# Stationary operands of the streamed products read with a step of two elements instead of one

## The chip, the core and the metric

The kernel runs on one core of a Trainium2 chip. The metric is the device time of one execution, in microseconds (us). The engines are TensorE (PE in the rows; PEld is its loading of stationary operands), VectorE (DVE), ScalarE (ACT), GpSimd (POOL) and SyncE (SP), which issues most of the DMAs. "Stationary operand" and "weights" mean the same below: the 128x128 block that TensorE holds while the columns of the moving operand stream past it.

## The reference

One inference step of a two-layer decoder, for a prompt of 256 tokens and 8 sequences of 4 new tokens (288 tokens in all), width 1024. Only the parts with streamed weights matter here:

```python
def mixer(h, st, lb, p):
    z = h @ p['w_in']
    ...
def peer(h, wq, k1, k2, u, v):
    ...
        sc, pos = lax.top_k(cand, PEER_TOPK)
        idx = jnp.take_along_axis(cidx, pos, axis=-1)
        gw = jax.nn.softmax(sc.astype(jnp.float32), axis=-1)
        act = jax.nn.gelu(jnp.einsum('thkd,td->thk', jnp.take(u, idx, axis=0), xb).astype(jnp.float32))
        return jnp.einsum('thk,thkd->td', (gw * act).astype(xb.dtype), jnp.take(v, idx, axis=0))
```

`peer_u` and `peer_v` have 16384 rows of 1024 floats for each layer. `w_in` has 26 blocks of 128 columns and 12 columns more.

## The kernel before

All weights come from one array in memory, `stream`, cut into tiles of 128 partitions by 1024 floats (512 KB). SyncE loads the tiles one after another into `ring` (three slots; the last stage has three more, `more_ring`). A loop over the two layers runs these stages in order: `project_block` (the product with `w_in`, 27 tiles, 288 moving columns), `local_block`, `hgrn_block` and `delta_block` (the three head groups), `output_block`, `experts_block` (128 tiles of `peer_u`; the prompt's 256 tokens are the moving columns, the result goes through gelu into a table of activations), `gates_block` (weights that table by the top-k gates) and `combine_block` (128 tiles of `peer_v`, moving operand the weighted activations of 128 experts for 256 tokens).

For the prompt, then, every expert is computed and the unwanted ones have gate zero. For the 32 sample tokens the wanted rows alone are gathered, by indirect DMAs from GpSimd, and VectorE multiplies and adds them; the sums stand in `m.tokens`, and 8 products with `m.folded` (line 2702) fold and turn them.

In `project_block`, `experts_block` and `combine_block` a float32 product is made of three products of type float32r. ScalarE copies half a tile (128x512) to `parts` as float32r, the high part (line 423 or 2631). VectorE or GpSimd writes what is left, the low part (line 430 or 2638). TensorE then multiplies: high weights by high and low moving operand (lines 473 and 2691), low weights by the high moving operand (lines 477 and 2695). `parts` has three places for a half tile, each with a high and a low side. Half a tile holds four chunks: chunk k is the 128x128 stationary operand for the k-th slice of the contraction (of the output, in `combine_block`). Each of the matmuls has its own load of a chunk, so each tile costs 24 loads and 24 matmuls.

Before the change chunk k of a half tile lies in 128 adjacent floats of each partition. The function `part` gives the view, and TensorE reads it with a step of one element. Each engine runs its instructions in the written order; semaphores join them (`hi_ready`, `lo_ready`, `done`, `parts_used`).

Of the kernel before, what the change touches and what calls it, by code (L numbers as in the profile page):

```python
# [27 lines left out]
P = 128  # L28
D = 1024
KD = D // P  # L30
DEPTH = 2
# [14 lines left out]
PARTS = 3  # L46
# [11 lines left out]
T_BETA = 0  # L58
T_IN = T_BETA + 1
T_LOCAL0 = T_IN + IN_TILES  # L60
# [5 lines left out]
T_U = T_QUERY + KD  # L66
T_V = T_U + NKEYS
T_X = T_V + NKEYS
# [44 lines left out]
NSAMP = NB * NS  # L113
# [284 lines left out]
def sum_column(pe, m, k, out):  # L398

    return pe.matmul(out, m.ones, m.square[:, k, :], start=(k == 0), stop=(k == KD - 1))  # L400
# [6 lines left out]

def part(m, q, side):

    return m.parts[:, q % PARTS, side, :].rearrange("p (k n) -> p k n", k=KD // 2)  # L410


def half_tile(m, t, half):
# [20 lines left out]
def wait_low(eng, m, s, first, g, j, half):  # L434

    t = first + j
    if half:
        eng.wait_ge(m.done[t % RING], g + (t // RING + 1))
    else:
        eng.wait_ge(s["lo_ready"], g * RING + (j + 1))  # L440


def each_tile(eng, first, end, body, ring=RING):

    assert first % ring == 0
    start, turns = first // ring, end // ring
    if turns - start == 1:
        for j in range(ring):
            body(start, j)
    elif turns > start:  # L450
        with eng.Fori(start, turns) as g:
            for j in range(ring):
                body(g, j)
    for n in range(turns * ring, end):
        body(turns, n % ring)


def split_product(pe, m, s, first, g, j, hr, out, tokens, columns=None):

    for half in range(2):
        hi, lo = part(m, 2 * j + half, 0), part(m, 2 * j + half, 1)
        pe.wait_ge(s["hi_ready"], g * 2 * RING + (2 * j + half + 1))
        for k in range(KD // 2):
            kk = half * KD // 2 + k
            if columns is not None:  # L470
                pe.wait_ge(columns, kk + 1)
            for side in range(2):
                pe.matmul(out, hi[:, k, :], hr[:, side, kk, 0:tokens], start=(kk + side == 0), stop=False)  # L473
        wait_low(pe, m, s, first, g, j, half)
        for k in range(KD // 2):
            kk = half * KD // 2 + k
            mm = pe.matmul(out, lo[:, k, :], hr[:, 0, kk, 0:tokens], start=False, stop=(kk == KD - 1))  # L477
        mm.then_inc(s["parts_used"], 1)


# [151 lines left out]
def project_block(nc, m, l, hr, stream, small_in, mixc_in, state_in):  # L632
# [7 lines left out]
    with signals(nc, m, names) as s, nc.psum_tensor("ps_z", [P, 4, 512], F32) as ps_z, \  # L640
# [101 lines left out]
        def _(v):  # L742
# [81 lines left out]
            for t in range(1, 1 + IN_TILES):  # L824
                for half in range(2):
                    split_low(v, m, s, T_BETA, 0, t, half)
                n = t - 1
                if n == CONV_AT - 2:
                    soft_in()
                elif n == CONV_AT:  # L830
                    v.wait_ge(s["pads_ready"], 4)
                if 0 <= n - CONV_AT < 4 * CONV:
                    part, k = (n - CONV_AT) // CONV, (n - CONV_AT) % CONV
                    v.wait_ge(s["z_out"], 3 * part + 4)
                    if part:
                        conv(m.yc, m.xc, range(3 * part - 3, 3 * part), k, m.par("dn_w"))
                    else:
                        conv(m.yb, m.xb, range(B_TILES), k, m.par("lru_w"), m.par("lru_b"))
                    if k == CONV - 1:
                        v.wait_ge(s["conv_step"], count[0])  # L840
                        v.sem_inc(s["conv_done"], 1)
                if n == CONV_AT + CONV:
                    v.tensor_copy(m.xcb[:, :, 0:NP], m.yb[:, :, 0:NP])
                    v.tensor_copy(batched(m.xcb[:, :, NP:NT]),
                                  m.yb[:, :, XP:XW].rearrange("p k (b s) -> p k b s", b=NB)[:, :, :, 0:NS])
                elif n == IN_TILES - 5:
                    soft_first()
                elif n == IN_TILES - 4:
                    soft_series(0, 3)
                elif n == IN_TILES - 3:  # L850
                    soft_series(3, len(LOG1P))
                elif n == IN_TILES - 2:
                    soft_last()
# [1344 lines left out]
def experts_block(nc, m, l, hr, stream, spots_in):  # L2198
# [7 lines left out]
    with signals(nc, m, names) as s, nc.psum_tensor("ps_s", [P, 4, 512], F32) as ps_s, \  # L2206
# [12 lines left out]
        def _(pe):  # L2219
            def tile(g, j):  # L2220
                pe.wait_ge(s["act_out"], g * RING + (j + 1))
                split_product(pe, m, s, T_U, g, j, hr, ps_u[:, j, 0:NP], NP)
# [368 lines left out]
def combine_block(nc, m, l, stream, u_rows):  # L2591

    AHEAD = 2
# [12 lines left out]
    with signals(nc, m, names) as s, \  # L2606
# [34 lines left out]
        def low_is_there(pe, g, j, half):  # L2641
            _, _, done, base = slot(j)
            if half:
                pe.wait_ge(done, g + (base + 1))
            else:
                pe.wait_ge(s["lo_ready"], g * VRING + (j + 1))

        def bank(n):
            return ps[:, 2 * n:2 * n + 2, :]
# [9 lines left out]
        @block.sync  # L2659
        def _(sp):  # L2660
            def load(g, j):
                tile, loaded, done, base = slot(j)
                sp.wait_ge(done, g + base)
                sp.dma_start(tile, stream[l, g * VRING + (T_V + j), :, :]).then_inc(loaded, 16)

            for j in range(RING, VRING):
                tile, loaded, _, _ = slot(j)
                sp.dma_start(tile, stream[l, T_V + j, :, :]).then_inc(loaded, 16)
            with sp.Fori(1, TURNS) as g:
                for j in range(VRING):  # L2670
                    load(g, j)
            for j in range(NKEYS % VRING):
                load(TURNS, j)

        @block.tensor
        def _(pe):
            pe.wait_ge(s["zeroed"], 1)
            for n in range(4):
                pe.matmul(bank(n), zeros[:, 0:P], zeros[:, :], start=True, stop=False)

            def tile(g, j):
                pe.wait_ge(s["act_hi"], g * VRING + (j + 1))
                for half in range(2):
                    q = (2 * j + half) % PARTS
                    hi, lo = part(m, q, 0), part(m, q, 1)
                    pe.wait_ge(s["hi_ready"], g * 2 * VRING + (2 * j + half + 1))
                    for side in range(2):
                        if side and half == 0:
                            pe.wait_ge(s["act_lo"], g * VRING + (j + 1))
                        for k in range(KD // 2):  # L2690
                            pe.matmul(ps[:, half * KD // 2 + k, :], hi[:, k, :], act_parts[:, j % AHEAD, side, :],  # L2691
                                      start=False, stop=False)
                    low_is_there(pe, g, j, half)
                    for k in range(KD // 2):
                        mm = pe.matmul(ps[:, half * KD // 2 + k, :], lo[:, k, :], act_parts[:, j % AHEAD, 0, :],  # L2695
                                       start=False, stop=False)
                    mm.then_inc(s["parts_used"], 1)

            each_tile(pe, 0, VRING * (TURNS - 1), tile, VRING)
            pe.wait_ge(s["samples_ready"], 1)  # L2700
            for k in range(KD):
                mm = pe.matmul(ps_m[:, NSAMP * k:NSAMP * (k + 1)], m.tokens[:, k * P:(k + 1) * P], m.folded,
                               start=True, stop=True)
            mm.then_inc(s["samples_summed"], 1)
            each_tile(pe, VRING * (TURNS - 1), NKEYS, tile, VRING)
            for n in range(4):
                pe.matmul(bank(n), zeros[:, 0:P], zeros[:, :], start=False, stop=True).then_inc(s["summed"], 1)
            for k in range(KD):
                pe.wait_ge(s["squares_ready"], k + 1)
                mm = sum_column(pe, m, k, ps_n[:, 0:NT])  # L2710
            mm.then_inc(s["sums_ready"], 1)
# [155 lines left out]
def host_layout(a):  # L2867
# [9 lines left out]
    stream = np.zeros((DEPTH, TILES, P, D), f)  # L2877
# [12 lines left out]
    out = a["w_out"].reshape(DEPTH, KD, P, 2, D // 2)[:, OUT_K].reshape(DEPTH, KD // 2, 2, P, 2, D // 2)  # L2890
    stream[:, T_OUT:T_QUERY] = out.transpose(0, 4, 1, 3, 2, 5).reshape(DEPTH, KD, P, D)
    stream[:, T_QUERY:T_U] = a["peer_wq"].reshape(DEPTH, KD, P, D)
    stream[:, T_U:T_V] = a["peer_u"].reshape(DEPTH, NKEYS, NKEYS, KD, P).transpose(0, 2, 4, 3, 1).reshape(DEPTH, NKEYS, P, D)
    stream[:, T_V:T_X] = a["peer_v"].reshape(DEPTH, NKEYS, NKEYS, D).transpose(0, 2, 1, 3)

    small = np.zeros((DEPTH, P, SMALL_W), f)

# [39 lines left out]
    j, i = np.arange(P)[:, None], np.arange(P)[None, :]  # L2937
# [89 lines left out]
```

## Time and profile before

| | |
|---|---|
| median of 3 runs | 2350.78 us (2343.35 to 2357.78) |
| the profiled execution's own time | 2358.03 us |
| its span, first to last instruction | 2356.1 us |
| mean granted TensorE clock | 0.971 of full |
| PE busy | 2249.4 us, 95% |
| PEld busy | 2085.2 us, 89% |
| DVE, ACT, POOL busy | 63%, 54%, 45% |

The profile describes one execution. Busy time of PE overlaps that of PEld, and neighbouring matmuls overlap each other, so that the mean duration of a matmul is longer than the time from one to the next. That distance is found from a stretch that holds nothing else: its length over the number of matmuls in it.

### The profile page before, as it was taken

The numbers are of one execution on the slowest core, as the hardware profiler recorded it, in microseconds if no ns is written. First come the engines' busy times: TensorE is split into PE (matmuls) and PEld (weight loads), VectorE is DVE, ScalarE is ACT, GpSimd is POOL, SyncE is SP. The second block draws the span as 40 slices with busy tenths as digits, with TensorE's granted clock in tenths as the row PEclk, the third lists the DMA queues.
The fourth block names the chain that finished last, engine by engine and source line by source line (L and its number), as shares of the span: only waits on it lengthen the run. The fifth ranks groups of instructions, "written<-read, shape, count | busy, mean of one in ns | idle before, by whom it ended". The sixth has DMA issues, their size and how long they took to land. (4 is left out here: it accounts for less than half of the span.)

```text
span 2356.1 us, 57811 instructions
## 1 busy us (share of the span) xinstructions
PE 2249.4 (95%) x20446; PEld 2085.2 (89%) x20478; DVE 1495.8 (63%) x3099; ACT 1271.2 (54%) x2439; POOL 1054.3 (45%) x960
## 2 busy tenths in 40 slices
PE   6979999999999999999989799999999999999998
PEld 4956779999998799999979377799999978999997
DVE  3756527963225968888666663499422287887885
ACT  3634215567557855555556431355765597555554
POOL 0021007874445746566300210288544474665661
PEclk9978899999999999999999789999999999999999
DMA  7462034555554179889644602355555533898993
GB/s 285 153 251 91 12 135 164 177 186 201 187 188 164 63 266 312 288 301 313 204 162 163 257 30 92 124 180 179 196 187 187 187 117 129 299 310 272 311 310 101
DMA packets 123814, 455.52 MB, mean 193 GB/s; under 512 B 13744, under 2 KB 14256, under 8 KB 122544
## 3 DMA queue, kind: packets, MB, share of 16 engines
q1 hardware_dynamic: 105264, 386.80, 46.4%
q0 software_dynamic: 18432, 67.12, 10.4%
q8 instruction: 78, 1.28, 0.2%
q14 instruction: 40, 0.33, 0.1%
HBM read 449.37 MB, written 4.49 MB: 193 GB/s over the span
## 5 line engine op out<-in xcount | busy, mean ns | idle before, releaser
L430 POOL TENSOR_TENSOR parts<-ring,parts 128x512 fp32r<-128x512 f32 x358 | 463.8, 1299 | 475.0 <-ACT parts L423 461.4
L423 ACT ACTIVATE parts<-ring 128x512 fp32r<-128x512 f32 x620 | 389.3, 632 | 348.4 <-PE ps_u L477 280.8
L473 PE MATMUL ps_u<-h_parts,parts 128*128 128x256 f32 x4096 | 563.0, 280 | 1.0 <-ACT parts L423 0.6
L2691 PE MATMUL ps_y<-act_parts,parts 128*128 128x256 f32 x4096 | 562.8, 279 | 0.0
L473 PEld LDWEIGHTS ps_u<-h_parts,parts 128*128 128x128 f32 x4096 | 514.4, 188 | 3.5 <-ACT parts L423 2.0
L2691 PEld LDWEIGHTS ps_y<-act_parts,parts 128*128 128x128 f32 x4096 | 515.1, 188 | 0.8 <-ACT parts L2631 0.7
L430 DVE TENSOR_TENSOR parts<-ring,parts 128x512 fp32r<-128x512 f32 x262 | 180.7, 693 | 372.0 <-ACT parts L423 350.5
L2740 POOL TENSOR_TENSOR act_parts<-big,act_parts 128x256 fp32r<-128x256 f32 x256 | 246.4, 962 | 303.5 <-ACT act_parts L2720 303.5
L477 PE MATMUL ps_u<-h_parts,parts 128*128 128x256 f32 x2048 | 322.2, 279 | 1.4 <-DVE parts L430 1.1
L2695 PE MATMUL ps_y<-act_parts,parts 128*128 128x256 f32 x2048 | 322.7, 279 | 0.0
L477 PEld LDWEIGHTS ps_u<-h_parts,parts 128*128 128x128 f32 x2048 | 275.4, 188 | 2.2 <-DVE parts L430 1.5
L2695 PEld LDWEIGHTS ps_y<-act_parts,parts 128*128 128x128 f32 x2048 | 275.5, 188 | 0.0
L2638 DVE TENSOR_TENSOR parts<-ring,parts 128x512 fp32r<-128x512 f32 x260 | 213.8, 845 | 74.1 <-ACT parts L2631 73.4
L2638 DVE TENSOR_TENSOR parts<-more_ring,parts 128x512 fp32r<-128x512 f32 x252 | 209.1, 849 | 73.7 <-ACT parts L2631 73.7
L2720 ACT ACTIVATE act_parts<-big 128x256 fp32r (+1 forms) x256 | 107.1, 418 | 220.4 <-PE ps_y L2695 211.0
L2631 ACT ACTIVATE parts<-ring 128x512 fp32r<-128x512 f32 x260 | 162.0, 624 | 49.9 <-PE ps_y L2695 49.9
L2631 ACT ACTIVATE parts<-more_ring 128x512 fp32r<-128x512 f32 x252 | 157.4, 625 | 45.8 <-PE ps_y L2695 45.8
L2526 POOL TENSOR_TENSOR onehot<-keep,sel 128x512 f32<-128x512 f32 x128 | 133.1, 1042 | 49.9 <-PE ps_g L2498 37.0
L2498 PEld LDWEIGHTS ps_g<-onehot 128*128 128x128 f32 x1024 | 135.6, 196 | 16.9 <-issue 13.2
L2498 PE MATMUL ps_g<-onehot 128*128 128x128 f32 x1024 | 140.6, 281 | 7.7 <-ACT onehot L2539 4.1
L473 PE MATMUL ps_z<-x_parts,parts 128*128 128x288 f32 x864 | 133.2, 296 | 4.5 <-ACT parts L423 4.5
L473 PEld LDWEIGHTS ps_z<-x_parts,parts 128*128 128x128 f32 x864 | 121.0, 188 | 5.8 <-ACT parts L423 5.4
(407 smaller groups left out, 2801.3 us busy)
## 6 DMA issues: line engine op xcount, KB each, us to landing
ring<-in_stream SPq DMA_DIRECT2D x506, 512.0 KB, 3.5
more_ring<-in_stream SPq DMA_DIRECT2D x126, 512.0 KB, 5.1
extra_ring<-in_stream SPq DMA_DIRECT2D x32, 512.0 KB, 5.4
mod_ring<-in_stream SPq DMA_DIRECT2D x32, 512.0 KB, 3.3
big<-in_stream SPq DMA_DIRECT2D x16, 512.0 KB, 11.6
out_state_out<-big SPq DMA_DIRECT2D x2, 1440.0 KB, 6.9
big<-in_state SPq DMA_DIRECT2D x2, 1280.0 KB, 10.6
big<-in_mixc SPq DMA_DIRECT2D x2, 1024.0 KB, 8.1
```

The costliest lines, as they stand in the source:

```text
L423: eng.activation(m.parts[:, q % PARTS, 0, :], half_tile(m, t, half), ACT.Copy).then_inc(s["hi_ready"], 1)
L430: eng.tensor_tensor(m.parts[:, q % PARTS, 1, :], half_tile(m, t, half), m.parts[:, q % PARTS, 0, :].bitcast(F32), ALU.subtract).then_inc(m ...
L473: pe.matmul(out, hi[:, k, :], hr[:, side, kk, 0:tokens], start=(kk + side == 0), stop=False)
L477: mm = pe.matmul(out, lo[:, k, :], hr[:, 0, kk, 0:tokens], start=False, stop=(kk == KD - 1))
L2498: mm = pe.matmul(ps_g[:, q % SETS, c, :], first[:, q % SETS, c, :], second[:, q % SETS, c, :], start=True, stop=True)
L2526: pool.tensor_tensor(second[:, g % SETS, :, :], spread(m.iota, 1, GROUP), spread(tokens_of(m.second_key, i, g), 2, P), ALU.subtract).then_ ...
L2631: act.activation(m.parts[:, q % PARTS, 0, :], tile[:, half * D // 2:(half + 1) * D // 2], ACT.Copy).then_inc(s["hi_ready"], 1)
L2638: v.tensor_tensor(m.parts[:, q % PARTS, 1, :], tile[:, half * D // 2:(half + 1) * D // 2], m.parts[:, q % PARTS, 0, :].bitcast(F32), ALU.s ...
L2691: pe.matmul(ps[:, half * KD // 2 + k, :], hi[:, k, :], act_parts[:, j % AHEAD, side, :], start=False, stop=False)
L2695: mm = pe.matmul(ps[:, half * KD // 2 + k, :], lo[:, k, :], act_parts[:, j % AHEAD, 0, :], start=False, stop=False)
L2720: act.activation(act_parts[:, j % AHEAD, 0, :], column(g, j), ACT.Copy).then_inc(s["act_hi"], 1)
L2740: pool.tensor_tensor(act_parts[:, j % AHEAD, 1, :], column(g, j), act_parts[:, j % AHEAD, 0, :].bitcast(F32), ALU.subtract).then_inc(s["ac ...
```

## The change

The host lays the streamed tiles of `w_in`, `peer_u` and `peer_v` out differently: the two chunks of a pair are interleaved, element by element. Where a partition held 128 floats of chunk 0 and then 128 of chunk 1, it now holds the first float of chunk 0, the first of chunk 1, the second of chunk 0, and so on. `part` returns the four chunks as views with a step of two floats. The copies that split a tile into high and low parts run over whole half tiles, with the same instructions as before, since the order inside does not matter to them; the tiles have the same size and the same loads. The gathered rows of `peer_v` come interleaved too, so that the sums in `m.tokens` are, and the last 8 products read them with the step of two (line 2702 before). `peer_u` rows for the gather come from another array and keep their order, and so do the other tiles (`w_out`, `peer_wq`, `w_ada`).

On no engine does the change add, drop or move an instruction; what differs is the access pattern of the stationary operands. In the kernel before, every one of them has a step of one element, or is four runs of 32 elements with that step (bfloat16).

```diff
 def part(m, q, side):
 
-    return m.parts[:, q % PARTS, side, :].rearrange("p (k n) -> p k n", k=KD // 2)
+    pairs = m.parts[:, q % PARTS, side, :].rearrange("p (j n b) -> p j n b", j=KD // 4, b=2)
+    return [pairs[:, k // 2, :, k % 2] for k in range(KD // 2)]
...
             for side in range(2):
-                pe.matmul(out, hi[:, k, :], hr[:, side, kk, 0:tokens], start=(kk + side == 0), stop=False)
+                pe.matmul(out, hi[k], hr[:, side, kk, 0:tokens], start=(kk + side == 0), stop=False)
...
-            mm = pe.matmul(out, lo[:, k, :], hr[:, 0, kk, 0:tokens], start=False, stop=(kk == KD - 1))
+            mm = pe.matmul(out, lo[k], hr[:, 0, kk, 0:tokens], start=False, stop=(kk == KD - 1))
...
+            tokens = m.tokens.rearrange("p (j n b) -> p j n b", j=KD // 2, b=2)
             for k in range(KD):
-                mm = pe.matmul(ps_m[:, NSAMP * k:NSAMP * (k + 1)], m.tokens[:, k * P:(k + 1) * P], m.folded,
+                mm = pe.matmul(ps_m[:, NSAMP * k:NSAMP * (k + 1)], tokens[:, k // 2, :, k % 2], m.folded,
                                start=True, stop=True)
...
+    for tiles in (slice(T_BETA, T_LOCAL0), slice(T_U, T_X)):
+        chunks = stream[:, tiles].reshape(DEPTH, -1, P, KD // 2, 2, P)
+        stream[:, tiles] = chunks.transpose(0, 1, 2, 3, 5, 4).reshape(DEPTH, -1, P, D)
```

The two products of `combine_block` change from `hi[:, k, :]` and `lo[:, k, :]` to `hi[k]` and `lo[k]` in the same way.

## Rows read from the trace of the kernel before

**Rows 1.** The page: busy time, share of the span and instructions of each engine

```profile
PE 2249.4 (95%) x20446; PEld 2085.2 (89%) x20478; DVE 1495.8 (63%) x3099; ACT 1271.2 (54%) x2439; POOL 1054.3 (45%) x960
```

**Rows 2.** Groups by line and form, PE: count, busy us, mean ns, idle us before

```profile
L473 PE MATMUL ps_u<-h_parts,parts 128*128 128x256 f32 x4096 | 563.0, 280 | 1.0 <-ACT parts L423 0.6
L2691 PE MATMUL ps_y<-act_parts,parts 128*128 128x256 f32 x4096 | 562.8, 279 | 0.0
L2695 PE MATMUL ps_y<-act_parts,parts 128*128 128x256 f32 x2048 | 322.7, 279 | 0.0
L477 PE MATMUL ps_u<-h_parts,parts 128*128 128x256 f32 x2048 | 322.2, 279 | 1.4 <-DVE parts L430 1.1
L473 PE MATMUL ps_z<-x_parts,parts 128*128 128x288 f32 x864 | 133.2, 296 | 4.5 <-ACT parts L423 4.5
L477 PE MATMUL ps_z<-x_parts,parts 128*128 128x288 f32 x432 | 75.4, 297 | 0.1
```

**Rows 3.** Busy us (x matmuls) in stretches of combine, project (layers 0, 1) and output

```profile
850.00:1150.00 300.00, 300.00 (x2572) 1.00 0.89 299
75.00:105.00 30.00, 30.00 (x229) 1.00 0.47 159
1215.00:1245.00 30.00, 30.00 (x228) 1.00 0.51 172
335.00:350.00 15.00, 15.00 (x63) 1.00 0.42 140
```

**Rows 4.** Groups by line and form, PEld: loads of 128, 32 and 12 columns

```profile
L2691 PEld LDWEIGHTS ps_y<-act_parts,parts 128*128 128x128 f32 x4096 | 515.1, 188 | 0.8 <-ACT parts L2631 0.7
...
L2254 PEld LDWEIGHTS ps_s<-keep,big 128*32 128x32 f32 x128 | 3.4, 110 | 0.3
...
L933 PEld LDWEIGHTS ps_q<-big 128*12 128x12 f32 x24 | 2.1, 92 | 3.8 <-issue 2.9
```

**Rows 5.** Timeline, PEld, 1161.5 to 1164.2 us: start us, length us, instructions

```profile
1161.93 1.87 PEld L2702 LDWEIGHTS ps_m<-keep,big 128*128 128x128 f32 x16
1163.72 0.65 PEld L2691 LDWEIGHTS ps_y<-act_parts,parts 128*128 128x128 f32 x5
```

**Rows 6.** Timeline, PE, same stretch: the matmuls of 32 columns to these loads

```profile
1162.05 1.87 PE L2702 MATMUL ps_m<-keep,big 128*128 128x32 f32 x16
```

**Rows 7.** Timeline, PE, 332 to 352 us: products of type f32 in the output stage

```profile
331.51 20.85 PE L2191 MATMUL ps_w<-big,ring 128*128 128x288 f32 x82
```

**Rows 8.** The page: groups that split the tiles, and what they wait for

```profile
L430 POOL TENSOR_TENSOR parts<-ring,parts 128x512 fp32r<-128x512 f32 x358 | 463.8, 1299 | 475.0 <-ACT parts L423 461.4
L423 ACT ACTIVATE parts<-ring 128x512 fp32r<-128x512 f32 x620 | 389.3, 632 | 348.4 <-PE ps_u L477 280.8
...
L2638 DVE TENSOR_TENSOR parts<-ring,parts 128x512 fp32r<-128x512 f32 x260 | 213.8, 845 | 74.1 <-ACT parts L2631 73.4
```

More of the change, by code:

```diff
@@ L2690, in tile @@
                         for k in range(KD // 2):
-                            pe.matmul(ps[:, half * KD // 2 + k, :], hi[:, k, :], act_parts[:, j % AHEAD, side, :],
+                            pe.matmul(ps[:, half * KD // 2 + k, :], hi[k], act_parts[:, j % AHEAD, side, :],
                                       start=False, stop=False)
@@ L2694, in tile @@
                     for k in range(KD // 2):
-                        mm = pe.matmul(ps[:, half * KD // 2 + k, :], lo[:, k, :], act_parts[:, j % AHEAD, 0, :],
+                        mm = pe.matmul(ps[:, half * KD // 2 + k, :], lo[k], act_parts[:, j % AHEAD, 0, :],
                                        start=False, stop=False)
```

## Prediction

> **What bounds the kernel now.** I began with the page's busy times [rows 1]: PE is busy for 95% of the span, PEld for 89%, and no other engine passes 63%. The groups by line and form come next [rows 2]. Two stages with the same form, 128x256, hold 4096+2048 matmuls in `experts_block` and as many in `combine_block`, 12288 together, and the project stage has 864+432 = 1296 of 288 columns. What the reader is to see there is the last column: TensorE idles 1.0, 0.0, 0.0 and 1.4 us before the four large groups, and 4.6 us before the two small ones. These matmuls wait for nobody. The splitting engines wait instead, POOL 461 us for ACT's high part and ACT 281 us for TensorE [rows 8]. So in these stages the time is the number of matmuls by the distance from one to the next.
>
> The means of 280 and 296 ns are not that distance, since matmuls overlap. The stretches give it [rows 3]. From 850 to 1150 us TensorE does 2572 matmuls in 300 us, 116.7 ns each (one or two of the count belong to the edges). In the project stage 229 and 228 in 30 us give 132 ns. The granted clock is 1.00 in all of them, that is 2.4 GHz. The changed matmuls are then 12288 x 116.7 ns = 1434 us, and 1296 x 132.2 ns = 171 us, 1605 of the 2356 us of the span. A nanosecond more or less for each is 13.6 us, or 0.6%. A change of one operand's reading can therefore matter a great deal, or not at all.
>
> **What a load costs now.** Each matmul has a load in front of it, which runs beside the matmul before. The question is how long it holds the path that it uses. Its mean duration is 188 ns for 128 columns, 110 ns for 32 and 92 ns for 12 [rows 4]. Between 12 and 128 columns that is 96 ns for 116 columns, 0.83 ns a column, and a fixed part which overlaps. So 128 columns hold the path for 106 ns. A second reading comes from the only place where loads of 128 columns meet short matmuls of 32 columns: the 16 of line 2702 start at 1161.93 us and the next load at 1163.72 [rows 5, 6], 111.9 ns from load to load. A load thus takes 106 to 112 ns and its cover is 116.7 ns. Only 4.8 to 10.7 ns are free beside 256 columns, and 20 to 26 ns beside 288. There is almost no cover: a slower load soon moves the end.
>
> **The change part by part.** Instructions, tiles, DMA sizes, the splits on ScalarE, VectorE and GpSimd, and their order stay as they are; these parts cost nothing because nothing in them differs, so no cover is needed. The waits stay too, with the same things queued behind them. What remains is one term: 12288 + 1296 loads, and the 32 of line 2702 (16 in each layer), read a float in every 8 bytes instead of one in every 4. The kernel before has no load with a step of two, so I bound its cost.
>
> The upper bound: the path delivers bytes, wanted or not, no faster than now. Then a column takes 1.66 ns, a load 212 ns, and the distance becomes 111.9+106 = 218 ns. That is +101.3 ns x 12288 = +1245 us, +85.8 ns x 1296 = +111 us, and 3 us for line 2702: +1359 us, 3710 us in all.
>
> The middle: the load is read as fast as the moving operand is. The moving side gets 256 columns of 4 bytes in 116.7 ns, 0.456 ns for 4 bytes. If the stationary side can have the same, 8 bytes for a column take 0.91 ns, and a load 117 ns instead of 106, which is 11 ns more. Of these the free 4.8 to 10.7 ns take a part: the distance grows by 0.3 to 6 ns, at most 72 us, nothing beside 288 columns.
>
> The lower bound of a cost is not zero. In the f32 stage 63 records of 288 columns stand in 15 us, 242 ns each [rows 3, 7], and each has one load. If such a record passes its columns twice, a pass takes 121 ns, 0.42 ns a column, one column a tick of 2.4 GHz. By that rate 256 float32r columns should take 107.6 ns and take 116.7; 288 should take 121 and take 132.2. Some 9 and 11 ns are lost in each, and no row says to what. If they come from loads and moving reads that get in each other's way, another reading pattern could give them back, or lose them again.
>
> **I take zero** for the term. Reasons: the load takes one column in 0.83 ns, whatever the memory could give, while the moving operand gets 4 bytes in 0.456 ns on the same kind of memory. The stationary side asks for half the rate of its neighbour; with the step doubled it spans about the same bytes a nanosecond as the moving side has all the time (8 in 0.83 ns against 8 in 0.91). The middle case is the row nearest to this change, and it comes within 6 ns of no cost. And the lost 9 ns don't behave as a collision with the load would: the load is the same for 288 columns, which still lose 2 ns more.
>
> The Trainium skill, page "SBUF — State Buffer", section "Door 1: The DMA port swizzle", says that reads come in lines of 16 bytes, that at least two accesses must hit a line for full bandwidth, and that each crossing to a new line costs something. A step of two floats has exactly two hits a line, so by the first half of the rule nothing changes. By the second half, lines change twice as often and the load could slow. No row here shows a stepped read on TensorE, so the trace can't say which half holds.
>
> **Rivals.** (a) Loads or moving reads get somewhat slower. For: the cover is only 4.8 to 10.7 ns, and the strided load spans 9.6 bytes a nanosecond where the moving side gets 8.8. Price at load's own rate +72 us, 2423 us. If the lost 9.1 and 11.2 ns are collisions and there are twice as many, the price is 12288 x 9.1 + 1296 x 11.2 ns = 112+15 = +127 us, 2478 us. It decides from the point where a load passes some 117 ns. Against: the growth with the columns, above.
>
> (b) The load takes twice its time: 3710 us. For: no row shows that skipped floats come free. Against: loads at 0.83 ns a column for 4 bytes leave half of what the moving side gets unused, so 4 bytes a column isn't their limit by memory.
>
> (c) Faster: the lost 9 ns are collisions between two readers that walk adjacent floats in step, and the new step breaks them up. Then experts gives 6144 x 9.1 ns = 56 us, project 15 us, combine up to 56 us. Others come into the way: POOL's two halves of a tile take 2 x 1299 = 2598 ns [rows 8] where TensorE's 24 matmuls take 24 x 116.7 = 2800 ns now and would take 2582; nearly nothing is left there. In combine the DMA engines are busy for 0.89 and move 299 GB/s [rows 3], and 8% more brings them to 0.96; I give that stage half, 28 us. Sum -99 us, 2252 us. For: a loss of 24 ticks that repeats. Against: the same growth with columns, and that the f32 records, with loads of the same form, lose only 1 ns.
>
> (d) That the change doesn't do what it says: if the loads were read by columns in another way than the program's, or in more records, the counts of loads would grow. The instructions are as many as before, so I leave it in the forecast's case.
>
> **How the numbers follow.** The sum is made against the profiled execution, 2358.03 us with a span of 2356.1; it is zero, so the prediction is the median of the runs, 2351 us. The forecast gets 0.66, (a) 0.12, (b) 0.09, (c) 0.13. With the forecast alone the range would be 2340 to 2365. To leave no more than 2 in 10 out it must take in (c) and the nearer price of (a), which is 2250 to 2425 us; (b) and the dearer end of (a) stay outside. Within 1%, 23.5 us, which is about what a measurement of this kernel can tell from no change, I put 0.66; faster 0.13; slower 0.21.
>
> **What would show it.** If right: the stretches of combine and project keep 116.7 and 132 ns a matmul, the group of L2691 loads stays at 188 ns, and the 16 loads of the `m.tokens` product still stand 112 ns apart. The last is the sharpest, since nothing else covers a load there: under (a) it grows to some 123 ns, with the loads' mean near 199, under (b) to 218 with a mean near 294. If the loads keep 188 ns and the distance still moves, up or down, the collisions of (a) or (c) are the cause, and PE's mean duration will move with it. The prediction fails if a float32r load isn't limited by 0.83 ns a column but by its memory, or if skipped floats cost TensorE a fetch each.

## The result: 1.7% slower, and the profile after

| | before | after |
|---|---|---|
| median of 3 runs | 2350.78 us | 2394.77 us (2390.74 to 2395.1) |
| ratio | | 1.0171, 95% interval 1.0141 to 1.0201 |
| span of the profiled execution | 2356.1 us | 2393.0 us |
| PE busy | 2249.4 us | 2288.4 us |

The page after, its busy times, answers to [rows 1]. Line numbers moved by one or two (L473 is now L474, L2691 is L2692, L2702 is L2704):

```profile
PE 2288.4 (96%) x20478; PEld 2124.2 (89%) x20478; DVE 1498.3 (63%) x3099; ACT 1271.6 (53%) x2439; POOL 1043.5 (44%) x960
```

DVE and ACT stayed within 3 us and POOL lost 11 us; PE gained 39.0 us, which is the whole difference of the spans (36.9 us) and close to that of the medians (44.0 us; the profiled execution before was 7 us slower than its median). PE and PEld have 20478 records each. Before, PE had 20446 and its loads 20478, some matmul records being missing there; no load was added.

The groups by line and form after, PE and PEld, answer to [rows 2, 4]:

```profile
L474 PE MATMUL ps_u<-h_parts,parts 128*128 128x256 f32 x4096 | 578.1, 285 | 0.5 <-ACT parts L424 0.3
L2692 PE MATMUL ps_y<-act_parts,parts 128*128 128x256 f32 x4096 | 577.7, 284 | 0.0
L474 PE MATMUL ps_z<-x_parts,parts 128*128 128x288 f32 x864 | 133.8, 297 | 4.4 <-ACT parts L424 4.4
```
```profile
L2692 PEld LDWEIGHTS ps_y<-act_parts,parts 128*128 128x128 f32 x4096 | 532.3, 196 | 0.7 <-ACT parts L2632 0.7
```

The reader is to see three things. The load's mean duration went from 188 to 196 ns, in the groups that read with a step. The matmul's went from 280 to 285 ns with 256 columns, but only from 296 to 297 with 288. And TensorE still waits for nobody (0.5 and 0.0 us). The time is lost inside its own stream.

The same stretch of combine before, then stretches of combine and project after, with busy PE (x matmuls), answer to [rows 3]. The last two lines are the matmuls and loads of experts alone, PE and PEld, before and after:

```profile
860.00:1140.00 280.00, 280.00 (x2401) 1.00 0.91 305
```
```profile
860.00:1140.00 280.00, 280.00 (x2335) 1.00 0.89 297
75.00:105.00 30.00, 30.00 (x226) 1.00 0.51 168
```
```profile
400.00:700.00 300.00, 296.29 (x2521) 294.83 (x2520) 0.00 (x0) 0.00 (x0) 1.00 0.56 187
400.00:700.00 300.00, 297.04 (x2459) 295.86 (x2459) 0.00 (x0) 0.00 (x0) 1.00 0.55 183
```

From one combine matmul to the next it was 280/2401 = 116.6 ns and is 280/2335 = 119.9 ns, 3.3 ns more. In experts busy PE for each matmul went from 296.29/2521 = 117.5 ns to 297.04/2459 = 120.8 ns, 3.3 ns more as well. The granted clock is 1.00 (2.4 GHz) in all. In the project stage 226 matmuls stand where 229 did, 132.7 ns against 131.0. The product with the summed tokens, whose loads nothing covers, on the timeline after (PEld), answers to [rows 5]:

```profile
1171.81 1.96 PEld L2704 LDWEIGHTS ps_m<-keep,big 128*128 128x128 f32 x16
1173.70 0.43 PEld L2692 LDWEIGHTS ps_y<-act_parts,parts 128*128 128x128 f32 x3
```

16 loads in 1.89 us, 118 ns each, where 112 ns stood before. The sum: 12288 x 3.3 ns = 40.6 us, 1296 x 1.7 ns = 2.2 us, 32 x 6 ns = 0.2 us, together 43 us, against 44.0 measured. So the price of one matmul accounts for the whole. It does not yet say where 3.3 ns come from: a load of 118 ns is only 1.3 ns longer than the 116.7 ns that the matmuls stood apart.

### The profile page after: what moved, and what is told of

Its sections match the earlier page's. It is cut to its first block and busy times, and to the rows that moved or that the text cites. A ratio compares the mean times of both kernels' runs of the same rounds, so it can differ in the third digit from the quotient of the medians.

```text
span 2393.0 us, 57843 instructions
## 1 busy us (share of the span) xinstructions
PE 2288.4 (96%) x20478; PEld 2124.2 (89%) x20478; DVE 1498.3 (63%) x3099; ACT 1271.6 (53%) x2439; POOL 1043.5 (44%) x960
## 5 line engine op out<-in xcount | busy, mean ns | idle before, releaser
L474 PE MATMUL ps_u<-h_parts,parts 128*128 128x256 f32 x4096 | 578.1, 285 | 0.5 <-ACT parts L424 0.3
L2692 PE MATMUL ps_y<-act_parts,parts 128*128 128x256 f32 x4096 | 577.7, 284 | 0.0
L474 PEld LDWEIGHTS ps_u<-h_parts,parts 128*128 128x128 f32 x4096 | 531.3, 196 | 2.6 <-ACT parts L424 1.3
L2692 PEld LDWEIGHTS ps_y<-act_parts,parts 128*128 128x128 f32 x4096 | 532.3, 196 | 0.7 <-ACT parts L2632 0.7
L2742 POOL TENSOR_TENSOR act_parts<-big,act_parts 128x256 fp32r<-128x256 f32 x256 | 235.3, 919 | 335.9 <-ACT act_parts L2722 335.9
L478 PE MATMUL ps_u<-h_parts,parts 128*128 128x256 f32 x2048 | 330.6, 285 | 0.2
L2696 PE MATMUL ps_y<-act_parts,parts 128*128 128x256 f32 x2048 | 330.6, 284 | 0.0
L478 PEld LDWEIGHTS ps_u<-h_parts,parts 128*128 128x128 f32 x2048 | 285.1, 196 | 0.6 <-POOL parts L431 0.6
L2696 PEld LDWEIGHTS ps_y<-act_parts,parts 128*128 128x128 f32 x2048 | 285.6, 196 | 0.0
L474 PE MATMUL ps_z<-x_parts,parts 128*128 128x288 f32 x864 | 133.8, 297 | 4.4 <-ACT parts L424 4.4
L474 PEld LDWEIGHTS ps_z<-x_parts,parts 128*128 128x128 f32 x864 | 122.5, 195 | 5.8 <-ACT parts L424 5.3
```

Source lines behind the costliest of these rows:

```text
L474: pe.matmul(out, hi[k], hr[:, side, kk, 0:tokens], start=(kk + side == 0), stop=False)
L478: mm = pe.matmul(out, lo[k], hr[:, 0, kk, 0:tokens], start=False, stop=(kk == KD - 1))
L2692: pe.matmul(ps[:, half * KD // 2 + k, :], hi[k], act_parts[:, j % AHEAD, side, :], start=False, stop=False)
L2696: mm = pe.matmul(ps[:, half * KD // 2 + k, :], lo[k], act_parts[:, j % AHEAD, 0, :], start=False, stop=False)
L2742: pool.tensor_tensor(act_parts[:, j % AHEAD, 1, :], column(g, j), act_parts[:, j % AHEAD, 0, :].bitcast(F32), ALU.subtract).then_inc(s["ac ...
```

## Experiments

Two theories stood at the start. **L**: the step makes the load itself longer, and the distance between matmuls is the larger of what the load and what the moving operand need. **C**: the load's reading collides with the moving operand's, and the step makes that worse.

**bench_steps.** A block of TensorE work alone is added between the last layer and the final norm; everything else is the kernel before. Its groups of 32 matmuls read the stationary operand from `parts` with different steps:

```diff
+        def cols(x, step, n=P):
+            return x[:, 0:step * n].rearrange("p (n b) -> p n b", b=step)[:, :, 0]
...
+            for i in range(32): pe.matmul(ps[:, i % 4, 0:256], cols(flat, 2), flat[:, 0:256], start=True, stop=True)
+            for i in range(32): pe.matmul(ps[:, i % 4, 0:256], cols(flat, 3), flat[:, 0:256], start=True, stop=True)
...
```

> The kernel before with a bench added in front of the last stage: groups of 32 float32r matmuls, each group with one step of the stationary operand (1, 2, 3, 4, 5, 6, 8, 16 elements) and 64 moving columns, then steps 1, 2, 3, 4, 8 with 256 moving columns, then loads of 64 columns with steps 1, 2, 4. With 64 moving columns the load alone should set the distance, as at the product with the summed tokens, where it went from 112 ns to 118 ns. Theory L (the load itself takes longer with a step, and the distance is the larger of load and moving operand): steps 1 and 2 give 112 and 118 ns with 64 columns and 117 and 120 ns with 256. Within it, if the spanned bytes set the time at the rate of step 2 (1024 bytes in 118 ns), steps 4, 8 and 16 give 236, 472 and 944 ns; if it is lines of 16 bytes, steps 4, 8 and 16 cost the same and more than step 2; if any step other than one costs a fixed 6 ns, all give 118 ns. Theory C (a collision of the load's reading with the moving operand's): with 64 columns the steps differ by a quarter of what they do with 256.

Its timeline, PEld, each row a group of 32 loads; the steps are 1, 2, 3, 4 (L2840 to L2843, 64 moving columns), then 2, 3, 4, 8 (L2849 to L2852, 256 moving columns), then 1, 2, 4 with loads of 64 columns:

```profile
2347.91 3.66 PEld L2840 LDWEIGHTS ps_bench<-parts 128*128 128x128 f32 x32
2351.50 5.72 PEld L2841 LDWEIGHTS ps_bench<-parts 128*128 128x128 f32 x32
2357.10 6.95 PEld L2842 LDWEIGHTS ps_bench<-parts 128*128 128x128 f32 x32
2363.93 7.56 PEld L2843 LDWEIGHTS ps_bench<-parts 128*128 128x128 f32 x32
...
2405.85 3.91 PEld L2849 LDWEIGHTS ps_bench<-parts 128*128 128x128 f32 x32
2409.68 5.62 PEld L2850 LDWEIGHTS ps_bench<-parts 128*128 128x128 f32 x32
2415.22 7.56 PEld L2851 LDWEIGHTS ps_bench<-parts 128*128 128x128 f32 x32
2422.68 7.83 PEld L2852 LDWEIGHTS ps_bench<-parts 128*128 128x128 f32 x32
2430.42 2.02 PEld L2853 LDWEIGHTS ps_bench<-parts 128*64 128x64 f32 x32
2432.36 2.00 PEld L2854 LDWEIGHTS ps_bench<-parts 128*64 128x64 f32 x32
2434.29 3.92 PEld L2855 LDWEIGHTS ps_bench<-parts 128*64 128x64 f32 x32
```

The start of the next row less the start of this one, over 32, gives the distance. Step 1 takes 112 ns, step 2 takes 120 ns, step 3 takes 173, step 4 takes 233 and step 8 takes 242. Half as many columns take 61, 60 and 119 ns. Before a verdict the clock must be looked at, since the groups with 64 moving columns lost it. The stretches, PEld:

```profile
2406.20:2409.40 3.20, 3.20 (x28) 1.00 0.00 0
2410.00:2415.00 5.00, 5.00 (x30) 1.00 0.00 0
2415.50:2422.50 7.00, 7.00 (x32) 1.00 0.01 2
2423.00:2430.00 7.00, 7.00 (x31) 1.00 0.00 0
```

The four groups with steps 2, 3, 4 and 8 ran at the full clock. The groups with 64 moving columns and steps from 3 on ran at 0.50 (1.2 GHz), as did more than half of the one with step 2. The steps at the full clock fall on one line if the load pays for units of 16 bytes, called lines here: 128 columns touch 64, 96 and 128 lines with steps 2, 3 and 4, and 118 (the tokens product), 173 and 233 ns are 1.84, 1.81 and 1.82 ns a line. Step 8 touches no more lines than step 4, and costs 4% more, not twice as much. So the load by spanned bytes without end is out, and so is a fixed price of any step. Against theory C stands that step two costs more where the moving operand is short (6 ns with 32 columns in the tokens product) than with 256 (3.3 ns). The groups at the lower clock bear this out: there step 3 took (2363.93 - 2357.10)/32 = 213 ns instead of 173, while step 4 took 233 ns, the same as at the full clock. So part of a load's time, 112 ns at one level and 213 at the other, goes with the clock, the 1.82 ns a line do not, and the longer one counts.

One group of this bench speaks against theory L at 256 columns, and it is the one nearest to the kernel before. With step 1 and 256 moving columns (L2848) the clock came back to 1.00 within the group, and from 2404.6 to 2405.8 us it was 1.00 throughout:

```profile
2404.53 1.39 PEld L2848 LDWEIGHTS ps_bench<-parts 128*128 128x128 f32 x11
```

The next group starts at 2405.85 us, so these 11 loads stood 120.0 ns apart, as far as those with step 2. The bench thus shows a longer load where the load is bare, but no price of the step of two at 256 columns, and it does not reproduce the kernel's 116.7 ns with step 1. It differs from the kernel in that both operands are read from the same place and each matmul starts a new sum; no run took that apart.

**bench_widths.** The same, with other widths, types and steps.

```diff
+            for i in range(32): pe.matmul(ps[:, i % 4, 0:288], cols(flat, 1), flat[:, 0:288], start=True, stop=True)
...
+            for i in range(32): pe.matmul(ps[:, i % 4, 0:288], cols(flat, 2), flat[:, 0:288], start=True, stop=True)
...
+            for i in range(32): pe.matmul(ps[:, i % 4, 0:256], cols(flat, 1), cols(flat, 2, 256), start=True, stop=True)
...
```

> The kernel before with another bench: step 1 with 128 to 512 moving columns of float32r, step 2 with 288 and 320, step 4 with 288 and 512; plain float32 with 32 moving columns and steps 1, 2, 3, 4, 8; bfloat16 with steps 1, 2, 4, 8; and a moving operand with steps 2 and 4. Theory L: the distance stays near 112 to 114 ns up to some 240 columns and then grows by 0.42 to 0.48 ns a column (132 ns at 288), and step 2 changes nothing at 288 and 320 columns (less than 1 ns), since the load of 118 ns is covered; plain float32 costs 112 and 118 ns with steps 1 and 2. Theory C: step 2 costs some 3 ns at 288 and 320 columns too, and the distance at step 1 lies 9 ns or more above the moving operand's own time at every width, 512 columns too.

Timeline, PEld. Step 1 with 128, 192, 224, 288, 320, 384 and 512 moving columns is L2840 to L2846; step 4 with 288 and with 512 columns is L2849 and L2850:

```profile
2356.15 3.66 PEld L2840 LDWEIGHTS ps_bench<-parts 128*128 128x128 f32 x32
...
2366.88 4.26 PEld L2843 LDWEIGHTS ps_bench<-parts 128*128 128x128 f32 x32
2371.08 4.72 PEld L2844 LDWEIGHTS ps_bench<-parts 128*128 128x128 f32 x32
2375.76 5.56 PEld L2845 LDWEIGHTS ps_bench<-parts 128*128 128x128 f32 x32
2381.30 7.20 PEld L2846 LDWEIGHTS ps_bench<-parts 128*128 128x128 f32 x32
...
2397.59 7.54 PEld L2849 LDWEIGHTS ps_bench<-parts 128*128 128x128 f32 x32
2405.04 7.67 PEld L2850 LDWEIGHTS ps_bench<-parts 128*128 128x128 f32 x32
```

The same bench, PE; 288 and 320 columns with step 1 are L2843 and L2844, with step 2 L2847 and L2848:

```profile
2366.98 4.39 PE L2843 MATMUL ps_bench<-parts 128*128 128x288 f32 x32
2371.21 4.85 PE L2844 MATMUL ps_bench<-parts 128*128 128x320 f32 x32
2375.90 5.74 PE L2845 MATMUL ps_bench<-parts 128*128 128x384 f32 x32
...
2388.77 4.43 PE L2847 MATMUL ps_bench<-parts 128*128 128x288 f32 x32
2393.04 4.86 PE L2848 MATMUL ps_bench<-parts 128*128 128x320 f32 x32
2397.73 7.62 PE L2849 MATMUL ps_bench<-parts 128*128 128x288 f32 x32
```

The distance is 112 ns at 128, 192 and 224 columns, flat: there the load sets it. From 288 on it is 131, 146, 173 and 227 ns, 0.44 to 0.46 ns a column: there the moving operand does. But the price is not in proportion to the columns: from 320 to 512 each further column costs 0.42 ns, on top of some 13 ns. This is the mark that theory C had named, a distance 9 ns or more above the moving operand's own time at every width, 512 too. Above 320 columns those 13 ns do not go with the columns, and what they are is not shown.

By the starts of the PE rows, step 2 leaves 320 columns where they were (146.6 ns with either step), but 288 columns go from 132.2 to 133.4 ns, though a load of 118 ns is well covered there. Theory L allowed less than 1 ns, theory C some 3 ns at both widths; neither is met. Step 4 costs 233 ns with 288 columns and 237 with 512, whose own time is 227; a collision that simply adds would have added to 227 what it added to 131. So the distance is the larger of the two times to within 3 or 4 ns, and the excess shows where the two are close: load and moving operand of 118 and 117 ns make 120 in the kernel, 118 and 132 make 133, 233 and 227 make 237, while 118 and 147 make 147. That the step-two distances lie where 13 ns and 0.42 ns a column would put them (estimates of 120, 133 and 147 ns, from the two widths above) and the kernel's 116.7 ns lie under it is a regularity without a shown cause.

**step_four.** The changed kernel with four chunks interleaved instead of two.

```diff
-    pairs = m.parts[:, q % PARTS, side, :].rearrange("p (j n b) -> p j n b", j=KD // 4, b=2)
-    return [pairs[:, k // 2, :, k % 2] for k in range(KD // 2)]
+    four = m.parts[:, q % PARTS, side, :].rearrange("p (n b) -> p n b", b=4)
+    return [four[:, :, k] for k in range(KD // 2)]
...
```

> The changed kernel with four chunks interleaved, so that a load reads with a step of four elements (16 bytes); nothing else differs. Theory L with spanned bytes: a load of 236 ns, distance 238 ns at 256 and 288 columns, 12288 x 121 + 1296 x 106 ns = +1624 us, 3975 us. Theory L with a fixed cost of a step: 2395 us as with step two. Theory C: twice to three times the 44 us of step two, 2440 to 2480 us.

Measured: 3912.34 us, ratio 1.6628 (1.658 to 1.6676). Stretches, PE, in project and in experts:

```profile
75.00:105.00 30.00, 30.00 (x130) 1.00 0.30 97
1400.00:1700.00 300.00, 300.00 (x1287) 1.00 0.48 149
```

300/1287 = 233.1 ns and 30/130 = 230.8 ns: both widths now run at the load's 233 ns, as the bench had it. 12288 x 116.4 + 1296 x 99 ns = 1559 us; the kernel took 1558 us more than the 2354.72 us that stood beside it. The expectation had 3975 us for a load that pays by spanned bytes (236 ns) and 2440 to 2480 us for theory C: with step four the load's own time makes the price, and a fixed price of a step and theory C as the whole explanation are out.

**project_only** and **experts_only** put the step of two into one stage alone. Their core:

```diff
+        if tokens == NT:
+            hi, lo = stepped(m, 2 * j + half, 0), stepped(m, 2 * j + half, 1)
...
+    for tiles in (slice(T_BETA, T_LOCAL0),):
...
```
```diff
+        of = plain_part if tokens == NT else part
+        hi, lo = of(m, 2 * j + half, 0), of(m, 2 * j + half, 1)
...
+    for tiles in (slice(T_U, T_V),):
...
```

> The kernel before with the step of two in the 27 tiles of the project stage alone, where 1296 matmuls have 288 moving columns. Theory L: the load of 118 ns is covered by the 132 ns of the matmul, 0 to +2 us, ratio 0.999 to 1.001. Theory C: 3.3 ns or more for each of 1296, +4 us or more, ratio 1.002; a difference that only the stretches can show, 132.2 ns against 135.5 ns.

> The kernel before with the step of two in the 256 tiles of the experts stage alone (6144 of the 12288 matmuls with 256 columns); project, combine and the product with the summed tokens read with a step of one. Theory L, 3.3 ns for each matmul wherever it stands: +20 us, ratio 1.0087. Rival: the 44 us come from combine, where the DMA engines are busiest (0.89 against 0.55), and this kernel gains or loses under 8 us, ratio below 1.0035.

Measured: project_only 2354.73 us beside 2354.72 for before, ratio 1.0005 (0.9986 to 1.0023); its two stretches of 30 us hold 226 and 227 matmuls, [rows 3] 229 and 228. That is 1 to 2 ns of 132, at most 2 us, which the interval can't show. Theory C's 3.3 ns or more are not reached, and theory L's zero is not quite met either, as in the bench. experts_only 2374.28 us beside 2352.48, ratio 1.0104 (1.008 to 1.0128), +21.8 us where +20 was expected. Its stretches, PE, in combine and in experts:

```profile
860.00:1140.00 280.00, 280.00 (x2389) 1.00 0.91 303
520.00:700.00 180.00, 180.00 (x1503) 1.00 0.57 189
```

Experts goes at 119.8 ns with the DMA engines busy for 0.57, where combine has 0.91, and combine, read with a step of one, is back near 117. So the step of two on these loads is what costs 3.3 ns a matmul in the kernel, and it costs the same whether the DMA engines are busy for 0.57 or 0.9. The distance with step one is itself not quite constant: the kernel before has 851 matmuls from 2050 to 2150 us, 117.5 ns.

**bench_more.** A third bench, with groups of 512 columns between the cases to keep the clock.

```diff
+            for i in range(32): pe.matmul(ps[:, i % 4, 0:256], cols(flat, 16), flat[:, 0:256], start=True, stop=True)
...
+            for i in range(32): pe.matmul(ps[:, i % 4, 0:512], cols(flat, 1), flat[:, 0:512], start=True, stop=True)
...
+            for i in range(32): pe.matmul(ps[:, i % 4, 0:128], cols(plain, 2), plain[:, 0:128], start=True, stop=True)
...
```

> The kernel before with a third bench, in which wide groups (512 columns) stand between the cases so that the granted clock stays at 2.4 GHz. Theory L with lines: a load of 128 float32 columns takes the larger of some 107 to 112 ns and 1.82 ns for each line of 16 bytes that it touches (bench_steps: 173 ns for 96 lines, 233 for 128). Steps 5, 6 and 16 then give 233 to 242 ns with 256 moving columns, not more than step 4. Rival: the time goes by the distance spanned beyond 16 bytes too, then steps 5, 6 and 16 give 292, 350 and 933 ns. Moving operand: 256 columns with steps 2 and 4 gave 227 and 233 ns; if it pays by units of 8 bytes, 0.91 ns each, steps 3 and 8 give 233 too and 128 columns with step 2 give 113 to 117 ns; if by lines of 16 bytes, step 8 is above 400 ns. Plain float32 with 128 columns: 112, 118 and 233 ns with steps 1, 2, 4. bfloat16: loads with steps 1 to 16 all covered by 256 columns at 109 ns; a bfloat16 moving operand with steps 1 and 2 at 109 ns, with step 4 (8 bytes) at 227 to 233 ns.

Stretches, PE, all at the full clock: steps 5, 6 and 16 of a float32r load; float32r moving operands with steps 3 and 8; plain float32 with 128 columns and loads of steps 1, 2, 4 (two records a product):

```profile
2370.00:2376.00 6.00, 6.00 (x29) 1.00 0.00 0
2377.00:2384.00 7.00, 7.00 (x32) 1.00 0.00 0
2385.00:2391.00 6.00, 6.00 (x28) 1.00 0.01 3
2403.00:2409.00 6.00, 6.00 (x28) 1.00 0.00 0
2410.00:2416.00 6.00, 6.00 (x29) 1.00 0.01 3
...
2460.00:2466.00 6.00, 6.00 (x56) 1.00 0.00 0
2467.00:2473.00 6.00, 6.00 (x53) 1.00 0.01 3
2475.00:2488.00 13.00, 13.00 (x57) 1.00 0.00 0
```

Each stretch counts one or two matmuls of its edges. Measured by the starts of the groups, steps 5, 6 and 16 take 228, 229 and 222 ns, a little under the 233 of step 4: beyond 16 bytes the step costs no more. The rival that distance counts further is out. Plain float32 behaves as float32r, 114, 118 and 231 ns with the edge of the group in it. bfloat16 loads with steps 1 to 16 all fit under 256 bfloat16 columns at 109 ns. A load of step 2 beside 192 columns, which alone need less, takes 118 to 119 ns by the starts of its group: the bare load once more, not 120.

**low_bf16.** If 116.7 ns are the bytes of the moving operand, as theory L has it, fewer bytes should gain. Here the step is one again, and half of the low products of experts and all those of combine take bfloat16 on both sides. The remainder that these products add is rounded to bfloat16, and the moving operand for it too.

```diff
+def low_part(m, q):
+
+    return m.low_ring[:, q % PARTS, D:D + D // 2]
...
+                mm = pe.matmul(out, low[:, k, :], m.h16[:, k, :], start=False, stop=(kk == KD - 1))
...
-                        mm = pe.matmul(ps[:, half * KD // 2 + k, :], lo[:, k, :], act_parts[:, j % AHEAD, 0, :],
+                        mm = pe.matmul(ps[:, half * KD // 2 + k, :], lo[:, k, :], act_16[:, j % AHEAD, :],
...
+                act.activation(act_16[:, j % AHEAD, :], column(g, j), ACT.Copy)
```

> The kernel before, step one, with fewer bytes on both sides of a part of the products: the low weights of all combine tiles and of the second half tiles of experts are written as bfloat16 and meet the high moving operand rounded to bfloat16 (one more copy of 128x256 a tile on ScalarE in combine, four more copies a layer on GpSimd ahead of experts). 2048 + 1024 matmuls. The rounding is of a term that is itself the small remainder. Theory L (116.7 ns is the time of 1024 bytes of moving operand, 0.456 ns for 4 bytes, and 2-byte columns go at 0.42 ns, 109 ns for 256 as in bench_widths): 3072 x 7.6 ns = -23 us, ratio 0.990. Theory C (the 9 ns are lost to collisions of neighbours whatever they read): within 5 us of before, ratio 0.998 to 1.002.

Measured: 2353.39 us beside 2352.48, ratio 1.0005 (0.9989 to 1.0021). No gain: theory L missed by its whole 23 us, and what theory C had forecast came. Its timeline, PE, in combine, half a tile being 8 float32r and 4 bfloat16 matmuls:

```profile
1000.32 1.18 PE L2710 MATMUL ps_y<-act_parts,parts 128*128 128x256 f32 x8
1001.34 0.61 PE L2714 MATMUL ps_y<-act,low_ring 128*128 128x256 bf16 x4
1001.71 1.18 PE L2710 MATMUL ps_y<-act_parts,parts 128*128 128x256 f32 x8
```

From 1000.32 to 1001.71 us is 1.39 us for 12, where 12 x 116.7 ns = 1.40. The four bfloat16 matmuls start within 0.37 us of each other and of the next float32r one, but the eight float32r ones take 1.02 us where 8 x 116.7 is 0.93. What the narrow type gives is lost again in the float32r part. A float32r load of 112 ns doesn't fit beside a bfloat16 matmul of 109, which may be why in part; no run took that apart. So the bytes of the moving operand do not set the time of this stream by themselves.

## Why the prediction was half right

The range of 2250 to 2425 us holds 2394.77, and the outcome was one to which it gave 0.21: slower by over 1%. The likeliest case, no change, did not occur.

**What bounds the kernel** was read rightly. TensorE's stream sets the time, a nanosecond a matmul is 13.6 us, and no other engine changed the end: 43 us of 44 follow from the distance between matmuls.

**What a load costs** was also right, and is the part that carried. Loads took 106 to 112 ns beside 116.7, and the tokens product was named as the place where a longer load shows bare. It showed 118 ns, and the loads' mean 196, where case (a) had said some 123 and 199. The 288 columns lost 1 to 2 ns; the 20 ns of cover had it at nothing.

**The step that failed is "I take zero".** The middle bound made the load 11 ns longer, which is 117 to 123 ns by its two readings (118 were measured), and priced the distance at 0.3 to 6 ns; it was 3.3. The prediction called that "within 6 ns of no cost" and rounded it to none, though its own factor makes 3.3 ns 44 us. The likeliest value of the term was the middle of that bound, 3.2 ns or 39 us, 2390 us. So the term was in the text, and its size was set wrongly. The fixed part was known as well: 111.9 ns was what loads took one after another, and to take 106 as the load and the rest as cover gave away most of the 5 ns that decide.

**The mechanism of the middle bound is shown in part only.** It says that what a load takes beyond its cover is added to the distance. A load of 118 ns passes a cover of 116.7 by 1.3 ns, which is 16 us. The other 2 ns of the 3.3, some 25 us, are not in it, and the bench, at 120.0 ns with either step, does not show them. That the middle of the bound fits so well is luck. No run shows where the 2 ns come from; the runs show that they come with the step of two in the kernel (experts_only, 21.8 us) and that load and moving operand of nearly the same length take 2 to 4 ns more than either.

**The argument for zero** was that the load takes 0.83 ns a column whatever the memory gives. It is true for step 1. With step 2 the 1.84 ns a line, 0.92 a column, are the slower of the two, by a tenth.

**The Trainium skill**, "SBUF — State Buffer", section "Door 1: The DMA port swizzle", asks for two accesses to a line of 16 bytes, and names four floats as the reach of a free stride. Two hits (step two) were nearly enough and not quite: +6 ns of 112, and here that decided. One hit (step four) cost double, 233 ns, so four floats are not free for the stationary operand. The runs agree with the line of 16 bytes, not with that reach: from step two on the load pays by the line. The measurement decides.

**The rivals.** (b), twice the time, fell for step two and is close to what step four does: its load takes 233 ns, where (b) had 218 for the distance. (c) and the dearer end of (a) rested on collisions behind the 9 ns lost at 256 columns, and on their number. They were not given back, and they did not double. What they are stays open: bench_widths has some 13 ns above 0.42 ns a column at 320 columns as at 512, so beyond 320 they do not grow with the columns, which weakens the argument against (a) and (c) that the prediction took from 256 and 288 columns. A mild form of (a), 2 ns a matmul beyond the longer load, is neither shown nor out. (d) fell by the equal count of loads.

## What to carry to other kernels

When TensorE loads new weights for each matmul, compare two times before touching the layout: the load's (here 112 ns for 128 float32 columns in a row, 118 with every second float, 233 with every fourth) and the moving operand's (117 ns for 256 float32r columns here, 131 for 288, 146 for 320, 227 for 512); the larger sets the distance, to within 4 ns, and at 256 columns they are 5 ns apart. Where they come close, don't trust the larger alone, but measure in the kernel itself: the bench of this case took 120 ns where the kernel took 117. Find the load's time where short moving operands leave it bare. And multiply a small bound by its count before rounding it to nothing: 3 ns were 1.7% of this kernel.

## What the runs showed of the hardware

- A load of 128 float32 or float32r columns takes the longer of about 112 ns and 1.82 ns for each line of 16 bytes it touches: 118, 173, 233 ns for steps 2, 3, 4 at the full clock. At the clock of 0.50 steps 3 and 4 took 213 and 233 ns: the part by the line did not slow down with the clock. Steps of 5, 6, 8 and 16 stay between 222 and 242 ns.
- At the full clock 256 float32r moving columns with a step of one take 117 ns in the kernel and 120 ns in bench_steps, and 227, 227, 233 and 218 ns with steps 2, 3, 4 and 8 (bench_widths and bench_more). The float32r moving operand doubles at a step of two floats already and then stays, where the load doubles at four. With bfloat16 256 moving columns took 113, 227 and 452 ns with steps 2, 4 and 8 (bench_more).
- Load and moving operand of nearly the same length take 2 to 4 ns more than the longer of them: 120 ns for 118 and 117 in the kernel, 237 ns for 233 and 227 in bench_widths.
- Matmuls of 64 moving columns in a row lost the clock: in bench_steps they began at 2347.9 us, and the granted clock was 0.50 from 2353 us on. Groups of 256 columns got it back to 1.00.
